# One copy and four transfers in place of four partition-shifting copies, for the rotary part of the queries

## What is computed

```
q = (_rms(c_q, norm_q[l]) @ w_uq[l]).reshape(B, L, N_HEADS, NOPE_DIM + ROPE_DIM)
q_n = q[..., :NOPE_DIM]
q_r = _apply_rope(q[..., NOPE_DIM:], cos[:, None, :], sin[:, None, :])
...
def _apply_rope(x, cos, sin):
    x1, x2 = jnp.split(x, 2, axis=-1)
    return jnp.concatenate([x1 * c - x2 * s, x2 * c + x1 * s], axis=-1)
```

## Time and profile before

| | |
|---|---|
| median of 3 runs | 1326.99 us (1325.7 to 1329.26) |
| the profiled execution | 1326.09 us, its span 1324.3 us |
| PE busy | 1283.4 us, 97% of the span |
| DVE, ACT, POOL busy | 688.6, 466.2, 328.4 us |
| chain that ended last, by engine | PE 87%, DVE 5%, ACT 4% |
| stretch in which the four pairs are prepared and computed | about 367 to 576 us |

### The profile page before, as it was taken

The page is one execution under the profiler, slowest core; times in us unless marked ns, Lnnn a source line. Parts: engine busy times, 40 slices in busy tenths (PEclk is TensorE's granted clock), DMA queues, the critical chain, the costliest instruction groups (busy, mean ns, idle before and its releaser), DMA issues.

```text
span 1324.3 us, 18183 instructions
## 1 busy us (share of the span) xinstructions
PE 1283.4 (97%) x7181; PEld 1112.1 (84%) x7181; DVE 688.6 (52%) x781; ACT 466.2 (35%) x689; POOL 328.4 (25%) x198
## 2 busy tenths in 40 slices
PE   5999999999999999989999999999999999999996
PEld 4888888888888888878888888888888888888885
DVE  4599999998868778774732131111111233343334
ACT  5211123532166665643621341222222323333325
POOL 1000000000043344327322222222222222223323
PEclk8999999999999999999999999999999999999998
DMA  5222222333210011123352212222222121111112
GB/s 181 64 64 63 63 73 64 100 112 103 87 52 21 21 33 32 32 84 111 96 206 92 64 48 64 61 62 62 61 62 63 61 78 64 64 64 64 64 48 96
DMA packets 123908, 96.18 MB, mean 73 GB/s; under 512 B 9695, under 2 KB 106013, under 8 KB 123852
## 3 DMA queue, kind: packets, MB, share of 16 engines
q1 hardware_dynamic: 121548, 89.12, 22.5%
q10 hardware_dynamic: 2304, 6.29, 1.4%
HBM read 85.96 MB, written 9.44 MB: 72 GB/s over the span
## 4 chain that ended last, share of the span: by engine, by line
PE 87%; DVE 5%; ACT 4%; issue 3%; DMA 1%; SPq 0%; POOL 0%; ACTq 0%; DVEq 0%
PE psum L319 56%; PE psum L1643 23%; PE psum L1520 3%; DVE acc L946 1%; PE psum L1550 1%; PE psum L1403 1%; DMA xt<-in_x_prompt 1%; PE psum L1532 1%; ACT junk L828 1%; ACT prob L611 1%; ACT pthi L618 1%; DVE ptlo L1031 0%; PE psum L1485 0%; DVE qt L1058 0%; PE psum L1650 0%
## 5 line engine op out<-in xcount | busy, mean ns | idle before, releaser
L303 POOL TENSOR_TENSOR wlo<-raw,whi 128x1024 fp32r<-128x1024 f32 (+1 forms) x105 | 240.6, 2292 | 865.4 <-ACT whi L298 865.4
L298 ACT ACTIVATE whi<-raw 128x1024 fp32r<-128x1024 f32 (+2 forms) x144 | 146.8, 1020 | 470.0 <-PE psum L319 255.0
L946 DVE SCALAR_TENSOR_TENSOR acc<-cs,convw,acc 128x799 f32<-128x799 f32 x232 | 243.1, 1113 | 0.0
L1222 DVE TENSOR_TENSOR hidlo<-hid,hidhi 128x1536 fp32r<-128x1536 f32 x32 | 82.2, 2569 | 169.7 <-ACT hidhi L806 169.7
L319 PE MATMUL psum<-uhi,wlo 128*128 128x512 f32 x592 | 152.7, 339 | 0.0
L319 PE MATMUL psum<-uhi,whi 128*128 128x512 f32 x592 | 152.1, 338 | 0.5 <-DVE wlo L303 0.5
L319 PE MATMUL psum<-ulo,whi 128*128 128x512 f32 x592 | 152.5, 338 | 0.0
L1643 PE MATMUL psum<-whi,hidhi 128*128 128x512 f32 x384 | 149.4, 389 | 0.0
L1643 PE MATMUL psum<-whi,hidlo 128*128 128x512 f32 x384 | 149.4, 389 | 0.0
L1643 PE MATMUL psum<-wlo,hidhi 128*128 128x512 f32 x384 | 149.4, 389 | 0.0
L1232 DVE SCALAR_TENSOR_TENSOR hid<-psum,rbc 128x768 f32 (+1 forms) x32 | 30.6, 958 | 216.6 <-PE psum L319 216.6
(11 more groups left out here) (223 smaller groups left out, 2068.2 us busy)
## 6 DMA issues: line engine op xcount, KB each, us to landing
raw<-in_w_in SPq DMA_DIRECT2D x38, 512.0 KB, 4.0
raw<-in_w_mlp_in SPq DMA_DIRECT2D x32, 512.0 KB, 4.0
raw<-in_w_mlp_out SPq DMA_DIRECT2D x32, 512.0 KB, 3.5
gates<-gout ACTq DMA_DIRECT2D x16, 384.0 KB, 2.4
gin<-gates SPq DMA_DIRECT2D x16, 384.0 KB, 3.0
raw<-in_w_o_attn SPq DMA_DIRECT2D x8, 512.0 KB, 3.9
raw<-in_w_conv_out SPq DMA_DIRECT2D x8, 512.0 KB, 3.9
raw<-in_w_out SPq DMA_DIRECT2D x8, 512.0 KB, 3.5
```

Source lines behind the costliest of these rows:

```text
L298: nc.scalar.activation(whi[:, c % 2, 0:w], raw[:, c % 4, 0:w], ACT.Copy).then_inc(hi_ready, 1)
L303: eng.tensor_tensor(out=wlo[:, c % 2, 0:w], in0=raw[:, c % 4, 0:w], in1=whi[:, c % 2, 0:w].bitcast(F32), op=ALU.subtract).then_inc(lo_read ...
L946: ins = nc.vector.scalar_tensor_tensor(out=a, in0=src, scalar=w, in1=a, op0=ALU.mult, op1=ALU.add)
L1222: nc.vector.tensor_tensor(out=hidlo[c % 2][:, :, :], in0=hid[:, ds(i * 8 + 2 * c, 2), :], in1=hidhi[c % 2][:, :, :].bitcast(F32), op=ALU.s ...
```

## The change

On ACT, the four shifting copies become one copy of the whole tile, PSUM to the last slab of `oraw`, and four transfers on ACT's own queue, each of 32 partitions by 768 columns (96 KB), from the copy to the exchanged quarter of `qsw`. A new semaphore `qr_copy` says that the copy is made; `qr_sw` now counts transfers (16 each, 64 for a pair). On DVE, the cosines multiply the copy in SBUF where they multiplied the PSUM tile, and wait for `qr_copy`. POOL's sines wait for all four transfers. PE's `keys` waits for `qr_copy` where it waited for the cosines (`qr_cos`), since the copy is now the last reader of the banks.

```diff
             def rotary_swap(p):
                 act.wait_ge(unit_used, p * 4 + (U_ATT + 1))
+                nc.scalar.activation(oraw[:, HEADS - 1], psum[:, 0, 0:TQ], ACT.Copy).then_inc(qr_copy, 1)
+                act.wait_ge(qr_copy, p + 1)
                 for b in range(4):
                     o = b ^ 1
-                    ins = nc.scalar.activation(qsw[32 * o:32 * o + 32, :], psum[32 * b:32 * b + 32, 0, 0:TQ], ACT.Copy)
-                ins.then_inc(qr_sw, 1)
+                    act.dma_start(qsw[32 * o:32 * o + 32, :], oraw[32 * b:32 * b + 32, HEADS - 1]).then_inc(qr_sw, 16)
...
             def rotary_cos(p):
-                dve.wait_ge(qr_sw, p + 1)
-                nc.vector.tensor_tensor(out=qt[:, 0:T_PROMPT], in0=psum[:, 0, 0:T_PROMPT], in1=rcos[:, 0:T_PROMPT], op=ALU.mult)
-                nc.vector.tensor_tensor(out=qt[:, T_PROMPT:TQ], in0=psum[:, 0, T_PROMPT:TQ], in1=rcos[:, SAMP0:TK], op=ALU.mult).then_inc(qr_cos, 1)
+                dve.wait_ge(qr_copy, p + 1)
+                nc.vector.tensor_tensor(out=qt[:, 0:T_PROMPT], in0=oraw[:, HEADS - 1, 0:T_PROMPT], in1=rcos[:, 0:T_PROMPT], op=ALU.mult)
+                nc.vector.tensor_tensor(out=qt[:, T_PROMPT:TQ], in0=oraw[:, HEADS - 1, T_PROMPT:TQ], in1=rcos[:, SAMP0:TK], op=ALU.mult).then_inc(qr_cos, 1)
...
             def start_pair(n):
-                gp.wait_ge(qr_sw, n + 1)
+                gp.wait_ge(qr_sw, n * 64 + 64)
...
-                        pe.wait_ge(qr_cos, p + 2)
+                        pe.wait_ge(qr_copy, p + 2)
                         keys(0, 0)
...
-            pe.wait_ge(qr_cos, 1)
+            pe.wait_ge(qr_copy, 1)
             keys(0, 0)
```

More of the change, by code:

```diff
@@ L243, in build @@
         v_mm, v_hi, v_lo = sem("v_mm"), sem("v_hi"), sem("v_lo")
-        qr_sw, qr_cos, qr_sin, qr_rot, qr_hi, qr_lo = (sem("qr_sw"), sem("qr_cos"), sem("qr_sin"),
+        qr_copy, qr_sw, qr_cos, qr_sin, qr_rot, qr_hi, qr_lo = (sem("qr_copy"), sem("qr_sw"), sem("qr_cos"), sem("qr_sin"),
                                                        sem("qr_rot"), sem("qr_hi"), sem("qr_lo"))
```

## The result

The changed kernel took 1333.97 us (median of 6 runs, 1331.77 to 1335.51) beside 1327.53 us for the kernel before on the same chip (6 runs). The ratio is 1.0045, its 95% interval 1.0035 to 1.0056: 6.0 us slower, 4.6 to 7.4. The profiled execution took 1334.55 us.

The account below looks back on a forecast made before the run. The prediction took PE's matmul stream, without slack at each pair's first scores, as the bound. Pairs 0 to 3 add 1.0 + 0.8 + 1.4 + 1.4 = 4.6 us, forecast 1331.1 us, own range 1329.7 to 1332.7, wide range 1327.6 to 1334.0.

Parts of the forecast that it names:

- PE has no slack, the tile's delay goes through: At each pair's first scores PE waits for `knlo`, 3.1 us in all; whatever delays `knlo` delays the kernel equally.
- The copy, 0.81 us, and the landing, 2.1 after the fourth issue: On ACT the whole-tile copy takes 0.81 us; the last transfer lands 2.1 us after issue, bounds 1.3 and 2.5.
- An issue, 0.45 us: On ACT's queue each transfer issue takes 0.45 us, so the tile is there 4.3 us after the exchange begins.
- Pair 0, +1.0: In pair 0 sines, `knlo` and first scores come 1.0 us later (0.2 to 1.4), with nothing to cover it.
- the rival of slow transfers: Transfers take 4 us from issue to landing; pair 0 +2.9, 8.2 us in all, 1334.8 us; chance 0.10.
- Pair 1, +0.8: In pair 1 the late sines alternate with the cosines after the taps, so the sum begins 0.8 us later (0.4 to 1.0).
- pairs 2 and 3, +1.4 each: In pairs 2 and 3 cosines taking turns with sines make the sum later by 1.3 or 1.7 us; 1.4 taken each.
- the order of the turns: DVE's cosines from SBUF and POOL's sines exclude each other and alternate instruction by instruction in pairs 1 to 3.
- The keys' wait of 1.15 us goes and reappears at `knlo`: In pair 1 PE's keys no longer wait 1.15 us for the cosines; first scores wait that much more for `knlo`.
- Taps of pair 1, 8.1 us: On DVE in pair 1 the taps take about 8.1 us instead of 9.37, with no sines between them.
- Made good later: ACT and DVE clear backlog during PE's wait, later score-loop waits shrink; half the delay, 2.3 us, remains, 1328.9 us; chance 0.10.
- faster: Tile lands within 1.2 us of issue and cosines pass beside sines, so pair 1's sum begins sooner; 1325.4 us; chance 0.05.

Follow-up runs that it names:

- load held: The changed kernel, with SP's weight load in pair 0 waiting until the four transfers have landed; 1332.77 us, 1.0030 of the kernel before.
- ACT copies the quarters: The changed kernel with four ACT copies from the SBUF copy in place of the four transfers; 1331.19 us, 1.0022 of the kernel before.
- one transfer: The changed kernel with one whole-tile transfer in place of four, exchange of quarters left out, cosines from the SBUF copy; 1334.36 us, 1.0043 of the kernel before.
- two queues: The changed kernel with two of each pair's four transfers issued by SP instead of ACT; 1334.51 us, 1.0036 of the kernel before.
- one transfer with PSUM cosines: The changed kernel with one whole-tile transfer, exchange left out, cosines reading PSUM and the keys waiting for them; 1331.19 us, 1.0025 of the kernel before.
- PSUM cosines: The changed kernel with the cosines reading the PSUM tile again and the keys waiting for them; 1331.24 us, 1.0024 of the kernel before.
- split first: The changed kernel, with POOL in pair 0 making the weight split before it waits for the sines' tile; 1333.35 us, 1.0039 of the kernel before.
- the change in pair 0: The kernel before with the change made in pair 0 alone, pairs 1 to 3 keeping their copies and cosines; 1331.43 us, 1.0030 of the kernel before.

## Why the prediction was right in direction and near in size

It said 4.6 us more; it is 6.0. The measured 1333.97 us lies above the range that the forecast gave itself (1329.7 to 1332.7) and 0.03 us inside the wide one (to 1334.0). The parts were less right than the sum: pair 0 was put 3.0 us too low and pairs 1 to 3 were put 2.0 us too high. That these errors cancel in part is luck: with only one of them put right the sum would have been 7.6 or 2.6 us.

- **PE has no slack, the tile's delay goes through.** Held. In pair 0 of the eight experiments that leave the split behind the sines and have a later tile, the first scores are late by the tile's delay, within 0.1 us (the tile's delay, then the scores'): 1.01 and 0.98, 1.61 and 1.57, 1.72 and 1.67, 2.52 and 2.45, 2.69 and 2.59, 3.29 and 3.19, 3.35 and 3.25, 3.63 and 3.53. Only the changed kernel pays more, 4.19 for 3.74: its half clock lasted the longest of all, and PE and no longer `knlo` set the time of its first scores.
- **The copy, 0.81 us, and the landing, 2.1 after the fourth issue.** Held outside pair 0: 0.81 and 2.2. **An issue, 0.45 us:** was 0.61 (2.44 for four). The tile came at 4.9, not 4.3.
- **Pair 0, +1.0.** The failed step: the landing was taken as 2.1 us in pair 0 too. It was 4.2, beside the weight load, as the rival of slow transfers had it for this pair (+2.9, a landing at 6.2), and a landing after 3 us was one of the signs of being wrong. It cost 4.2 us to the first scores and 0.6 behind them. With the load held the last transfer landed in 2.2. By the ratios pair 0 is 4.0 of 6.0 us, where the prediction had 1.0 of 4.6. That the values' wait would exceed PE's own, and that the clock then halves, was not seen: the text let them "come 1.0 later too, inside PE's own wait".
- **Pair 1, +0.8; pairs 2 and 3, +1.4 each.** Were 0.25, 1.1 and 0.95; timed as one, 1.6 us. The failed step is the order of the turns. The prediction let cosines and sines alternate piece by piece. The two cosines ran one behind the other and the sines stood still, and not only because the tile came at 4.9: with quarters copied by ACT the sines of pairs 2 and 3 arrived at 4.3, 0.1 us behind the first cosines, and again both cosines went first. The sign that it named as its refutation, cosines of 0.4 and 0.68 us in pairs 2 and 3, is there. Its price of 3.6 us for the turns was, however, nearly that of the kernel with one transfer, 3.4 (1.65, 0.91 and 0.87).
- **The keys' wait of 1.15 us goes and reappears at `knlo`.** Held in pair 1: no such row is left, and its wait for `knlo` is 1.73 where it was 0.56. The forecast total of about 9 us under `knlo` is 4.6, in three waits and not four, since pair 0's wait stands under the values instead (3.5 us).
- **Taps of pair 1, 8.1 us.** Were 8.31.
- **Made good later; faster.** Neither shows: the stretches from first scores to the next exchange are not shorter.

## What to carry to other kernels

A transfer that replaces copies of an engine is priced by where it ends: four issues from one queue (0.6 us each), its landing (2.2 us), and what else is in flight at that moment. This is to be done for each place, since the same four lines had the tile there at 4.9 us in the loop and at 6.0 to 7.1 in front of it. Two costs on one chain are to be tried together and apart: here a later tile made the engine conflict cheaper, so that undoing the lateness alone (two queues, one transfer) gave nothing in pairs 1 to 3, and undoing the conflict alone gave 1.5 us of 2.3. And ask of each stall of PE whether the clock comes back with it.

## What was not expected of the hardware

- **Idle time and the clock.** In pair 0 PE idled 3.54, 3.42, 3.07, 3.73, 2.48 and 2.27 us in six profiles, and the granted clock went to 0.50 in each: a microsecond before the idle time ended in the changed kernel, and up to 1.5 us behind its end in others. After waits of 0.9 to 1.65 us in this pair it did not fall. After 3.01 us, in the profile of one transfer with PSUM cosines, it stayed at 1.00 too:

```profile
376.00:378.00 2.00, 0.83 (x7) 0.83 (x8) 2.00 (x2) 0.03 (x1) 1.12 (x1) 1.00 0.00 0
378.00:380.00 2.00, 2.00 (x19) 2.00 (x18) 1.94 (x3) 1.95 (x3) 0.00 (x0) 1.00 0.45 131
```

So an idle stretch like this makes a fall likely, not certain. That profile is of an execution whose span is 1327.3 us, where its kernel's median is 1331.19; part of the spread between executions may be this. In pair 1 of the kernel with two queues the clock was 0.50 from 435 to 438 us, after waits of 1.7 us and, 5.8 us later, 1.8 us.

- **Who gets the turn.** Sines that arrived during an ordinary tap went before the next one (2.04 us in the earlier trace rows). Sines that arrived during the last tap, as much as 0.8 us before its end (ACT copies the quarters, pair 1: 3.01 us), lost to both cosines. And second sines directly behind first ones won against them (1.23 above). The taps wait for one another by a semaphore and the cosines only for the copy, made long before; that this decides is a guess.
- **Landings in pair 0.** The same four transfers beside the same load had the tile there at 7.06, 6.95, 6.35 and 6.01 us in four profiles (the changed kernel, PSUM cosines, split first, the change in pair 0). In the first two every issue took 0.6 us and the last transfer 4.2 and 4.1 us from issue to landing; in the others the fourth issue took 1.49 and 1.22 us, and the last landing 3.4 and 3.2. What differs between them stays open, as does the part of the instruction packet.
